# Weight halves made two blocks at a time: one ScalarE and one VectorE operation over two neighbouring blocks in the expert-mixture stage

## The chip, the cores and the metric

The kernel runs on one core of a Trainium2 chip. The metric is the device time in microseconds of one execution; the times shown are medians over runs of the same program. The profile is of one execution and is read in microseconds from the start of its span.

## What is computed

The whole kernel is two model blocks on 256 tokens of width 1024. The change is in the last stage, a mixture of 8 experts in which each token is sent to its best two:

```python
def moe_swiglu(h, router, wg, wu, wd):
    t = h.reshape(B_ * S_, D_)
    logits = (t @ router).astype(jnp.float32)
    top_v, top_i = lax.top_k(logits, TOP_K)
    gates = jax.nn.softmax(top_v, axis=-1)
    gate_full = jnp.sum(jax.nn.one_hot(top_i, N_EXPERTS, dtype=jnp.float32) * gates[..., None], axis=1)
    out = jnp.zeros_like(t)
    for e in range(N_EXPERTS):
        out = out + gate_full[:, e:e + 1].astype(t.dtype) * swiglu(t, wg[e], wu[e], wd[e])
    return out.reshape(B_, S_, D_)
```

`swiglu(h, wg, wu, wd)` is `(silu(h @ wg) * (h @ wu)) @ wd`, with 1024 x 3584 gate and up weights and 3584 x 1024 down weights for each expert, all float32.

## The kernel before

`stage_moe` works in passes. A pass gathers the rows of up to 128 tokens of one expert and streams that expert's weights from memory. There are `NE` = 8 passes and, for an expert with more than 128 tokens, an extra one; nine run with these inputs. A pass has 7 groups of 512 hidden columns; each group has 4 gate, 4 up and 4 down blocks, so `PASS` = 84 blocks of 128 x 1024 floats (512 KB). `ORDER` sets their order: gate 0, up 0, then for each further group g: gate g, up g, down g-1, and at last down 6. Blocks 80 to 83 are down 6.

A float32 product is made of three matmuls in the faster format `F32R`: each operand is split into a high half and the rest. For the weights this is done on the chip. `SP` loads a block into `raw`, a ring of `RING` = 21 slots. ScalarE's `high` (line 3610) copies it to `hi`, rounded, and VectorE's `low` (line 3783) writes `raw - hi` to `lo`. Both halves have `HALVES` = 6 buffers. TensorE (lines 3543 for gate and up, 3561 for down) reads them in 6 matmuls of 512 columns a block and adds one to `used`. `hi_ready`, `lo_ready` and `used` count blocks: `high` of block n waits for its load and for `used` of block n-6, `low` waits for `hi_ready`, TensorE and the reload of the ring slot wait for `lo_ready`.

Each engine runs its own program, in the order in which it is written. Between the halves stand the steps that tie groups together. ScalarE: `silu` writes `sg` (line 3625, with a load of its function table in the first group of a pass), `turned` writes `ah` (3629), `outputs` writes `y` (3636), `gathered` writes `hEh` (3620). VectorE: `product` writes `prod` (3788), `turned` writes `al` (3792), `places` (3815 to 3819, once a pass, after the up blocks of group 1, with two operations of 3737 behind it), `gathered` writes `hEl` (3778). TensorE: `turn` transposes `prod` (3550) and `down` waits for `al`; `who` (3531) stands between gate 0 and up 0; a pass's first matmul waits for `hEl`. The first `PRE` = 2 blocks of a pass are prepared at the end of the pass before: on ScalarE and VectorE block 0 of the next pass stands ahead of the last group's `turned`, block 1 behind it.

Of the kernel before, what the change touches and what calls it, by code (L numbers as in the profile page):

```python
# [7 lines left out]
ACT = mybir.ActivationFunctionType  # L8
ALU = mybir.AluOpType
# [9 lines left out]
T = 256  # L19
# [2092 lines left out]
HALVES = (slice(0, HD), slice(HD, P))  # L2112
# [1254 lines left out]
def stage_moe(nc, k, choice, w, hT, xn, x_tok, rows, out):  # L3367
# [10 lines left out]
    KINDS, UNITS = 3, 4  # L3378
    GATE, UP, DOWN = range(KINDS)
# [5 lines left out]
    PASS = GROUPS * KINDS * UNITS  # L3385
    RING, HALVES, PRE = 21, 6, 2
    ORDER = [(GATE, 0), (UP, 0)]
    for g in range(1, GROUPS):
        ORDER += [(GATE, g), (UP, g), (DOWN, g - 1)]
    ORDER.append((DOWN, GROUPS - 1))  # L3390
    AT_UNIT = {what: n * UNITS for n, what in enumerate(ORDER)}
    with Stage(nc, "moe") as st:
        sb, ps, sem = st.sb, st.ps, st.sem
        raw = sb("raw", [P, RING, D])
        hi, lo = sb("hi", [P, HALVES, D], F32R), sb("lo", [P, HALVES, D], F32R)
# [9 lines left out]
        hrow, gidx, gidx_ready, h_loaded = sb("hrow", [P, D]), sb("gidx", [P, 1], U32), sem("gidx_ready"), sem("h_loaded")  # L3405
# [4 lines left out]
        chosen, first, second = sb("chosen", [P, TT, NE]), sb("first", [P, TT, NE]), sb("second", [P, TT, NE])  # L3410
# [33 lines left out]
        with nc.Block() as block:  # L3444
# [157 lines left out]
            @block.scalar  # L3602
            def _(act):
                act.nop().then_inc(silu_ready, 1)
                act.activation(xh[:], xn[:], ACT.Copy).then_inc(xh_ready, 1)

                def high(p, n):
                    act.wait_ge(raw_loaded[n % RING], p * (PASS // RING * 16) + (n // RING * 16 + 16))
                    act.wait_ge(used, p * PASS + n + 1)
                    act.activation(hi[:, n % HALVES], raw[:, n % RING], ACT.Copy).then_inc(hi_ready, 1)  # L3610

                for n in range(PRE):
                    act.wait_ge(raw_loaded[n], 16)
                    act.activation(hi[:, n], raw[:, n], ACT.Copy).then_inc(hi_ready, 1)
                act.wait_ge(d_ready, 1)
                act.activation(e[:], df[:], ACT.Exp).then_inc(e_ready, 1)

                def gathered(p):
                    act.wait_ge(gather_psum, 2 * p + 2)
                    act.activation(hEh[:].rearrange("p k t -> p (k t)"), pX[:].rearrange("p b n -> p (b n)"), ACT.Copy).then_inc(hEh_ready, 1)  # L3620

                def silu(p, g):
                    act.wait_ge(used, AHEAD_USED + p * PASS + (AT_UNIT[GATE, g] + UNITS))
                    act.wait_ge(prod_ready, p * GROUPS + g + 1)
                    act.activation(sg[:], pB[:, GATE], ACT.Silu).then_inc(silu_ready, 1)

                def turned(p, g):
                    act.wait_ge(t_psum, p * GROUPS + g + 1)
                    act.activation(ah[:], pT[:], ACT.Copy).then_inc(ah_ready, 1)  # L3629

                def outputs(p):

                    act.wait_ge(used, AHEAD_USED + p * PASS)
                    act.wait_ge(y_free, p + 1)
                    act.wait_ge(idx_ready, p + 1)
                    act.activation(y[:].rearrange("p (h n) -> p h n", h=2), pY[:], ACT.Identity, scale=tokg[:, 1:2]).then_inc(y_ready, 1)

                def one(p):
                    for n in range(PRE, PASS):
                        high(p, n)  # L3640
                        if n == UNITS:
                            outputs(p)
                        kind, g = ORDER[(n - UNITS - 1) // UNITS]
                        if n >= 2 * UNITS and (n - UNITS - 1) % UNITS == UNITS - 1 and kind == GATE:
                            silu(p, g)
                            if g:
                                turned(p, g - 1)
                    high(p + 1, 0)
                    turned(p, GROUPS - 1)
                    for n in range(1, PRE):  # L3650
                        high(p + 1, n)
                    gathered(p + 1)

                act.wait_ge(gather_psum, 1)
                act.activation(hEh[:, 0:KD // 2].rearrange("p k t -> p (k t)"), pX[:, 0], ACT.Copy).then_inc(half_ready, 1)
                act.wait_ge(gather_psum, 2)
                act.activation(hEh[:, KD // 2:KD].rearrange("p k t -> p (k t)"), pX[:, 1], ACT.Copy).then_inc(hEh_ready, 1)

                def last(p):
# [37 lines left out]
            def _(dve):  # L3697
# [50 lines left out]
                for n in range(PRE):  # L3748
                    dve.wait_ge(hi_ready, n + 1)
                    dve.tensor_tensor(lo[:, n], raw[:, n], hi[:, n], ALU.subtract).then_inc(lo_ready, 1)  # L3750

                c.tick(dve.tensor_scalar(over[:], slot[:, :, 0:NE], float(P), None, ALU.subtract))
                c.link(dve.tensor_copy(wides[:], wide[:]))
# [24 lines left out]
                    dve.tensor_tensor(hEl[:].rearrange("p k t -> p (k t)"), pX[:].rearrange("p b n -> p (b n)"),  # L3778
                                      hEh[:].rearrange("p k t -> p (k t)"), ALU.subtract).then_inc(h_ready, 1)

                def low(p, n):
                    dve.wait_ge(hi_ready, p * PASS + n + 1)
                    dve.tensor_tensor(lo[:, n % HALVES], raw[:, n % RING], hi[:, n % HALVES], ALU.subtract).then_inc(lo_ready, 1)  # L3783

                def product(p, g):
                    dve.wait_ge(silu_ready, p * GROUPS + g + 2)
                    dve.wait_ge(used, AHEAD_USED + p * PASS + (AT_UNIT[UP, g] + UNITS))
                    dve.tensor_tensor(prod[:], pB[:, UP], sg[:], ALU.mult).then_inc(prod_ready, 1)

# [21 lines left out]
                def places(p):  # L3811

                    dve.wait_ge(m_psum, p + 1)
                    dve.wait_ge(y_free, p + 2)
                    dve.tensor_copy(tokg[:], pM[:, 0:3]).then_inc(ch2, 1)
                    dve.wait_ge(ch2, 2 * p + 1)
                    dve.scalar_tensor_tensor(out=idxf[:], in0=tokg[:, 2:3], scalar=unfilled[:, 1:2], in1=tokg[:, 0:1], op0=ALU.mult, op1=ALU.add).then_inc(ch2, 1)
                    dve.wait_ge(ch2, 2 * p + 2)
                    dve.tensor_tensor(idx[:], idxf[:], unfilled[:, 0:1], ALU.add).then_inc(idx_ready, 1)

                def one(p):
                    for n in range(PRE, PASS):
                        low(p, n)
                        kind, g = ORDER[(n - UNITS) // UNITS]
                        if n >= UNITS and kind == UP and (n - UNITS) % UNITS == UNITS - 1:
                            product(p, g)
                            if g == 1:
                                places(p)
                                gather_matrix(p + 1)
                            if g == 3:  # L3830
                                dve.wait_ge(a_psum, p + 1)
                                dve.tensor_scalar(gidx[:], pM[:, 4:5], float(T - 1), None, ALU.min).then_inc(gidx_ready, 1)
                        kind, g = ORDER[(n - UNITS - 1) // UNITS]
                        if n > UNITS and g and kind == GATE and (n - UNITS - 1) % UNITS == UNITS - 1:
                            turned(p, g - 1)
                    low(p + 1, 0)
                    turned(p, GROUPS - 1)

                    def others():
                        for n in range(1, PRE):  # L3840
                            low(p + 1, n)
                    gathered(p + 1, others)

                choices()
# [435 lines left out]
```

## Time and profile before

| | |
|---|---|
| median of 3 runs | 3125.44 us |
| lowest and highest of them | 3112.82 and 3127.72 us |
| span of the profiled execution | 3118.3 us |
| busy in the span: TensorE, weight loads, VectorE, ScalarE | 95%, 79%, 75%, 56% |
| mean granted TensorE clock | 0.974 |

The profile gives the profiled execution's span alone, from its first to its last instruction; it has no separate device time, so the span is what stands for it, and it is 7.1 us below the median of the runs. The halves are split from 2008.9 us on, and the last matmuls that read them start at 3107.8 us: the expert mixture is the last third of the span. TensorE's busy time is made of matmuls that overlap (a matmul of 512 columns lasts 0.39 us, the next one starts some 0.23 us after it), so a stall is best seen in what an engine waited for.

### The profile page before, as it was taken

To read this page: it belongs to the slowest core of one execution; us is meant where nothing else is said; L and a number is where in the kernel's file an instruction comes from. 1 tells how busy PE (TensorE), PEld (TensorE's weight loads), DVE (VectorE), ACT (ScalarE), POOL (GpSimd) and SP (SyncE) were. 2 spreads that over 40 slices of the span, in tenths; PEclk is the share of its full clock that TensorE was granted. 3 is DMA by queue.
4 is the path that set the end of the run, shared out by engine and by line. 5 is a ranking of instruction groups with operands and counts; after the bars stand their busy time and mean duration, and the time that the engine had idled before them with its cause. 6 is when DMAs were issued, how large, how long until landed. Compare 5 with 4: busy or idle time off the path is not lost. (4 is left out here: it accounts for less than half of the span.)

```text
span 3118.3 us, 52434 instructions
## 1 busy us (share of the span) xinstructions
PE 2962.4 (95%) x18296; PEld 2464.1 (79%) x18297; DVE 2341.3 (75%) x3606; ACT 1735.2 (56%) x2188; POOL 61.8 (2%) x69
## 2 busy tenths in 40 slices
PE   7999898999999999988899988899999999999999
PEld 3796547889888999977779877688888888888887
DVE  5675754889788666666655567699999998998998
ACT  4354303336533444446344363388888888888886
POOL 0000000000000000000000000000000000000000
PEclk9999899999999999999899998899999999999999
DMA  8570323444777666642145231499999999999995
GB/s 307 212 253 20 130 120 97 147 158 183 271 250 227 220 205 212 205 152 85 56 173 194 87 128 57 161 412 412 382 372 374 375 374 373 376 381 364 389 372 212
DMA packets 228409, 738.75 MB, mean 237 GB/s; under 512 B 23783, under 2 KB 60056, under 8 KB 225432
## 3 DMA queue, kind: packets, MB, share of 16 engines
q1 hardware_dynamic: 222648, 704.49, 61.7%
q0 software_dynamic: 5312, 31.98, 3.3%
q8 instruction: 85, 1.39, 0.2%
q14 instruction: 76, 0.62, 0.1%
q10 hardware_dynamic: 288, 0.26, 0.0%
HBM read 707.28 MB, written 29.36 MB: 236 GB/s over the span
## 5 line engine op out<-in xcount | busy, mean ns | idle before, releaser
L3783 DVE TENSOR_TENSOR moe_lo<-moe_raw,moe_hi 128x1024 fp32r<-128x1024 f32 x756 | 887.5, 1222 | 66.7 <-ACT moe_hi L3610 47.6
L3610 ACT ACTIVATE moe_hi<-moe_raw 128x1024 fp32r<-128x1024 f32 x756 | 791.0, 1061 | 155.4 <-PE moe_pB L3543 89.3
L3543 PE MATMUL moe_pB<-moe_hi,moe_hEh 128*128 128x512 f32 x1008 | 399.2, 396 | 0.3 <-DVE moe_hEl L3848 0.3
L3543 PE MATMUL moe_pB<-moe_hi,moe_hEl 128*128 128x512 f32 x1008 | 393.1, 390 | 0.0
L3543 PE MATMUL moe_pB<-moe_lo,moe_hEh 128*128 128x512 f32 x1008 | 392.7, 390 | 0.0
L3543 PEld LDWEIGHTS moe_pB<-moe_hi,moe_hEl 128*128 128x128 f32 x1008 | 189.3, 188 | 41.0
L3543 PEld LDWEIGHTS moe_pB<-moe_hi,moe_hEh 128*128 128x128 f32 x1008 | 189.3, 188 | 39.3 <-issue 1.7
L3543 PEld LDWEIGHTS moe_pB<-moe_lo,moe_hEh 128*128 128x128 f32 x1008 | 189.5, 188 | 37.6
L3561 PE MATMUL moe_pB<-moe_hi,moe_ah 128*128 128x512 f32 x504 | 197.1, 391 | 5.6 <-DVE moe_al L3792 5.6
L1971 PE MATMUL exp_pO<-exp_vh,exp_ah 128*128 128x512 f32 x512 | 200.1, 391 | 1.8 <-DVE exp_al L2056 1.8
L1971 PE MATMUL exp_pO<-exp_vl,exp_ah 128*128 128x512 f32 x512 | 200.0, 391 | 0.0
L1971 PE MATMUL exp_pO<-exp_vh,exp_al 128*128 128x512 f32 x512 | 199.2, 389 | 0.0
L3561 PE MATMUL moe_pB<-moe_hi,moe_al 128*128 128x512 f32 x504 | 196.3, 389 | 0.0
L3561 PE MATMUL moe_pB<-moe_lo,moe_ah 128*128 128x512 f32 x504 | 196.1, 389 | 0.0
L1996 ACT ACTIVATE exp_vh<-value_ring 128x1024 fp32r<-128x1024 f32 x128 | 134.7, 1055 | 103.5 <-PE exp_pO L1971 81.6
L2045 DVE TENSOR_TENSOR exp_vl<-value_ring,exp_vh 128x1024 fp32r<-128x1024 f32 x128 | 156.4, 1222 | 30.5 <-ACT exp_vh L1996 28.6
L2005 ACT ACTIVATE exp_ge<-exp_pS 128x256 f32<-128x256 f32 x64 | 24.5, 383 | 217.7 <-PE exp_pS L1959 217.7
L1959 PE MATMUL exp_pS<-fh,exp_ul 128*128 128x256 f32 x512 | 144.9, 283 | 0.0
L1959 PE MATMUL exp_pS<-fl,exp_uh 128*128 128x256 f32 x512 | 144.9, 283 | 0.0
L1959 PE MATMUL exp_pS<-fh,exp_uh 128*128 128x256 f32 x512 | 144.5, 282 | 0.0
L1621 PE MATMUL route_pS<-fh,route_uh 128*128 128x256 f32 x416 | 122.7, 295 | 8.4 <-DVE route_ul L1730 8.1
L2052 DVE TENSOR_TENSOR exp_at<-exp_ge,exp_gs 128x256 f32<-128x256 f32 x64 | 27.3, 426 | 128.5 <-ACT exp_ge L2005 114.6
(814 smaller groups left out, 6641.3 us busy)
## 6 DMA issues: line engine op xcount, KB each, us to landing
moe_raw<-in_moe_w SPq DMA_DIRECT2D x758, 512.0 KB, 6.5
value_ring<-in_peer_v SPq DMA_DIRECT2D x128, 512.0 KB, 4.4
key_ring<-in_peer_u SPq DMA_DIRECT2D x64, 512.0 KB, 3.6
exp_us<-in_peer_u SPq DMA_DIRECT2D x64, 512.0 KB, 5.1
inp_w<-in_w_mod SPq DMA_DIRECT2D x48, 512.0 KB, 7.6
inp_w<-in_w_tiles SPq DMA_DIRECT2D x40, 512.0 KB, 6.2
gates<-route_big POOLq DMA_DIRECT2D x8, 2048.0 KB, 7.3
exp_gs<-gates SPq DMA_DIRECT2D x32, 512.0 KB, 5.7
```

The lines of the kernel that those rows point to most:

```text
L1621: m = pe.matmul(pS[:, n % 2, 0:T], w, x[:, kd], start=kd == 0 and q == 0, stop=kd == KD - 1 and q == 2)
L1959: m = pe.matmul(pS[:, j % 2, 0:T], w, x[:, kd], start=kd == 0 and q == 0, stop=kd == KD - 1 and q == 2)
L1971: m = pe.matmul(pO[:, a, h], w[:, j % RING, ts], x, start=False, stop=False, skip_group_check=True)
L1996: act.activation(vh[:, j % RING], vs[:, j % RING], ACT.Copy).then_inc(vh_ready, 1)
L2005: act.activation(ge[:, j % 2], pS[:, j % 2, 0:T], ACT.Gelu).then_inc(ge_ready, 1)
L2045: dve.tensor_tensor(vl[:, j % RING], vs[:, j % RING], vh[:, j % RING], ALU.subtract).then_inc(vl_ready, 1)
L2052: dve.tensor_tensor(at[:].rearrange("p (c t) -> p c t", c=runs), scored.rearrange("p (c t) -> p c t", c=runs), gs[:, j // 4, :, j % 4], AL ...
L3543: i = pe.matmul(pB[:, kind], l[:, kd], m[:, n % HALVES, ns], start=kd == 0 and x == 0, stop=kd == KD - 1 and x == 2)
L3561: i = pe.matmul(pY[:, h], l[:, u], m[:, n % HALVES, hs], start=g == 0 and u == 0 and x == 0, stop=g == GROUPS - 1 and u == UNITS - 1 and x ...
L3610: act.activation(hi[:, n % HALVES], raw[:, n % RING], ACT.Copy).then_inc(hi_ready, 1)
L3783: dve.tensor_tensor(lo[:, n % HALVES], raw[:, n % RING], hi[:, n % HALVES], ALU.subtract).then_inc(lo_ready, 1)
```

## The change

`SPANS` cuts a pass into pairs of neighbouring blocks. Two blocks make a pair where both slots of `raw` and both buffers of `hi` and `lo` lie side by side, that is where neither ring wraps between them. A pass gets 40 pairs and 4 singles (blocks 20, 23, 62 and 65). One `high` and one `low` work on the whole span: `high` waits for both loads and for `used` of the span's last block less six, and the semaphores go up by two at its end. What stood behind a block now stands behind its span. At the end of a pass both first blocks of the next one are a pair behind `turned`. TensorE's program and that of `SP` are as they were.

```diff
+    SPANS, n = [], 0
+    while n < PASS:
+        both = n % RING < RING - 1 and n % HALVES < HALVES - 1
+        SPANS.append((n, 2 if both else 1))
+        n += SPANS[-1][1]
...
-                def high(p, n):
-                    act.wait_ge(raw_loaded[n % RING], p * (PASS // RING * 16) + (n // RING * 16 + 16))
-                    act.wait_ge(used, p * PASS + n + 1)
-                    act.activation(hi[:, n % HALVES], raw[:, n % RING], ACT.Copy).then_inc(hi_ready, 1)
+                def high(p, span):
+                    n, count = span
+                    for b in range(n, n + count):
+                        act.wait_ge(raw_loaded[b % RING], p * (PASS // RING * 16) + (b // RING * 16 + 16))
+                    act.wait_ge(used, p * PASS + n + count)
+                    act.activation(hi[:, n % HALVES:n % HALVES + count], raw[:, n % RING:n % RING + count], ACT.Copy).then_inc(hi_ready, count)
...
-                    for n in range(PRE, PASS):
-                        high(p, n)
-                        if n == UNITS:
-                            outputs(p)
...
-                    high(p + 1, 0)
+                    for first, count in SPANS[1:]:
+                        high(p, (first, count))
+                        for n in range(first, first + count):
+                            if n == UNITS:
+                                outputs(p)
...
                     turned(p, GROUPS - 1)
-                    for n in range(1, PRE):
-                        high(p + 1, n)
+                    high(p + 1, SPANS[0])
                     gathered(p + 1)
...
-                def low(p, n):
-                    dve.wait_ge(hi_ready, p * PASS + n + 1)
-                    dve.tensor_tensor(lo[:, n % HALVES], raw[:, n % RING], hi[:, n % HALVES], ALU.subtract).then_inc(lo_ready, 1)
+                def low(p, span):
+                    n, count = span
+                    dve.wait_ge(hi_ready, p * PASS + n + count)
+                    dve.tensor_tensor(lo[:, n % HALVES:n % HALVES + count], raw[:, n % RING:n % RING + count],
+                                      hi[:, n % HALVES:n % HALVES + count], ALU.subtract).then_inc(lo_ready, count)
...
-                    low(p + 1, 0)
                     turned(p, GROUPS - 1)
 
                     def others():
-                        for n in range(1, PRE):
-                            low(p + 1, n)
+                        low(p + 1, SPANS[0])
                     gathered(p + 1, others)
```

VectorE's program at the end of a pass, before: blocks 82 and 83 of the pass, block 0 of the next, the last `al`, block 1 of the next, `hEl`.

```order
L3783 TENSOR_TENSOR moe_lo<-moe_raw,moe_hi 128x1024
L3782 REGISTER_ALU
L3783 TENSOR_TENSOR moe_lo<-moe_raw,moe_hi 128x1024
L3782 ISA
L3783 TENSOR_TENSOR moe_lo<-moe_raw,moe_hi 128x1024
L3792 TENSOR_TENSOR moe_al<-moe_pT,moe_ah 128x512
L3774 ISA
L3782 REGISTER_ALU
L3783 TENSOR_TENSOR moe_lo<-moe_raw,moe_hi 128x1024
L3778 TENSOR_TENSOR moe_hEl<-moe_pX,moe_hEh 128x1024
```

The same place of the change: the pair 82 and 83, the last `al`, the pair 0 and 1 of the next pass, `hEl`.

```order
L3791 TENSOR_TENSOR moe_lo<-moe_raw,moe_hi 128x2048
L3801 TENSOR_TENSOR moe_al<-moe_pT,moe_ah 128x512
L3781 ISA
L3790 ISA
L3791 TENSOR_TENSOR moe_lo<-moe_raw,moe_hi 128x2048
L3785 TENSOR_TENSOR moe_hEl<-moe_pX,moe_hEh 128x1024
```

Of the three single `lo` ahead of the last `al`, the two of this pass have become one operation, and block 0 of the next pass has moved behind `al`.

VectorE's program of the change after the up blocks of group 1, behind the pair 18 and 19, `product` and the three operations of `places`: the two operations for `Pg`, single block 20, the pair 21 and 22, single block 23.

```order
L3745 TENSOR_SCALAR moe_Pg<-choice_io,moe_slot 128x128
L3745 REGISTER_ALU
L3745 TENSOR_SCALAR moe_Pg<-choice_io,moe_slot 128x128
L3790 REGISTER_ALU
L3791 TENSOR_TENSOR moe_lo<-moe_raw,moe_hi 128x1024
L3790 REGISTER_ALU
L3791 TENSOR_TENSOR moe_lo<-moe_raw,moe_hi 128x2048
L3790 REGISTER_ALU
L3791 TENSOR_TENSOR moe_lo<-moe_raw,moe_hi 128x1024
```

Before, the same steps stood between single blocks 19 and 20; now they stand between a pair and a single, with the next pair right behind.

## Rows read from the trace of the kernel before

**Rows 1.** The page's span and its busy time by engine, with share and instructions.

```profile
span 3118.3 us, 52434 instructions
...
PE 2962.4 (95%) x18296; PEld 2464.1 (79%) x18297; DVE 2341.3 (75%) x3606; ACT 1735.2 (56%) x2188; POOL 61.8 (2%) x69
```

**Rows 2.** 100 us in the MoE stage: each engine's busy time, clock, DMA.

```profile
2500.00:2600.00 100.00, 99.57 (x452) 82.49 (x453) 90.65 (x89) 83.11 (x86) 4.59 (x4) 1.00 0.98 369
```

**Rows 3.** Who waited for whom from 2100 to 3090 us: total us, times, longest.

```profile
ACT moe_hi L3610 <- PE moe_pB L3543: 82.9, 297, 0.3
...
DVE moe_lo L3783 <- ACT moe_hi L3610: 43.9, 89, 1.5
...
PE moe_pB L3561 <- DVE moe_al L3792: 5.0, 8, 0.6
```

**Rows 4.** Tile `moe_hi`, whole run: duration in ns (min/median/max), first and last start.

```profile
L3610 ACT ACTIVATE moe_hi<-moe_raw x756: 1043/1062/1069, 2024.0 to 3101.5; 128x1024 fp32r<-128x1024 f32 x189
L3783 DVE TENSOR_TENSOR moe_lo<-moe_raw,moe_hi x756: 1215/1222/1232, 2025.1 to 3102.5; 128x1024 fp32r<-128x1024 f32 x189
```

**Rows 5.** The page's group of `down`'s first matmuls: busy, mean ns, idle before and its releaser.

```profile
L3561 PE MATMUL moe_pB<-moe_hi,moe_ah 128*128 128x512 f32 x504 | 197.1, 391 | 5.6 <-DVE moe_al L3792 5.6
```

**Rows 6.** Tile `dense_uh` of the dense stage: the same two operations at 2048 columns.

```profile
L3963 ACT ACTIVATE dense_uh<-dense_us x21: 1903/1915/1917, 1594.3 to 1764.4; 128x2048 fp32r<-128x2048 f32 x21
L3993 DVE TENSOR_TENSOR dense_ul<-dense_us,dense_uh x21: 2291/2292/2293, 1596.2 to 1766.3; 128x2048 fp32r<-128x2048 f32 x21
```

**Rows 7.** The end of a pass: start us, duration us, engine, line, operation, idle before.

```profile
2492.89 0.39 PE L3561 MATMUL moe_pB<-moe_hi,moe_ah 128*128 128x512 f32 x1
...
2493.09 1.06 ACT L3610 ACTIVATE moe_hi<-moe_raw 128x1024 fp32r<-128x1024 f32 x1 [0.30 <-PE moe_pB L3543]
...
2498.34 0.60 PE L3550 MATMUL moe_pT<-ident,moe_prod 128*128 128x128 f32 x4
...
2498.97 0.60 ACT L3629 ACTIVATE moe_ah<-moe_pT 128x512 fp32r<-128x512 f32 x1 [0.73 <-PE moe_pT L3550]
...
2499.60 0.69 DVE L3792 TENSOR_TENSOR moe_al<-moe_pT,moe_ah 128x512 fp32r<-128x512 f32 x1
...
2500.43 0.49 PE L3561 MATMUL moe_pB<-moe_hi,moe_ah 128*128 128x512 f32 x1 [0.62 <-DVE moe_al L3792]
```

**Rows 8.** The turn of the same pass into the next one, the same columns.

```profile
2500.41 1.02 ACT L3620 ACTIVATE moe_hEh<-moe_pX 128x1024 fp32r<-128x1024 f32 x1
...
2501.45 1.28 ACT L3610 ACT_TABLE_LOAD   x1
...
2506.01 0.39 PE L3543 MATMUL moe_pB<-moe_hi,moe_hEh 128*128 128x512 f32 x1
...
2511.23 0.64 PEld L3531 LDWEIGHTS moe_pM<-moe_meta,moe_Pg 128*128 128x128 f32 x4
...
2511.81 0.49 PE L3543 MATMUL moe_pB<-moe_hi,moe_hEh 128*128 128x512 f32 x1
...
2513.01 0.60 ACT L3625 ACTIVATE moe_sg<-moe_pB 128x512 f32<-128x512 f32 x1
```

**Rows 9.** VectorE alone around `places` in the next pass, the same columns.

```profile
2528.97 0.69 DVE L3788 TENSOR_TENSOR moe_prod<-moe_pB,moe_sg 128x512 f32<-128x512 f32 x1 [0.29 <-PE moe_pB L3543]
...
2530.54 10.30 DVE L3783 TENSOR_TENSOR moe_lo<-moe_raw,moe_hi 128x1024 fp32r<-128x1024 f32 x9
```

**Rows 10.** The first blocks of the first pass, all engines, the same columns.

```profile
2024.03 2.96 ACT L3610 ACTIVATE moe_hi<-moe_raw 128x1024 fp32r<-128x1024 f32 x3 [0.95 <-PE moe_pB L3588]
...
2024.28 0.50 PE L3543 MATMUL moe_pB<-moe_hi,moe_hEh 128*128 128x512 f32 x1 [0.29 <-DVE moe_hEl L3848]
...
2025.12 3.50 DVE L3783 TENSOR_TENSOR moe_lo<-moe_raw,moe_hi 128x1024 fp32r<-128x1024 f32 x3 [1.08 <-ACT moe_hi L3610]
...
2027.13 0.39 PE L3543 MATMUL moe_pB<-moe_hi,moe_hEh 128*128 128x512 f32 x1
```

**Rows 11.** Tile `moe_raw`: from issue to landing of a block's load.

```profile
DMA to landing us min/median/max: 3.6/6.5/18.8
```

More of the change, by code:

```diff
@@ L3605, in _ @@
                 act.activation(xh[:], xn[:], ACT.Copy).then_inc(xh_ready, 1)
-                def high(p, n):
-                    act.wait_ge(raw_loaded[n % RING], p * (PASS // RING * 16) + (n // RING * 16 + 16))
-                    act.wait_ge(used, p * PASS + n + 1)
-                    act.activation(hi[:, n % HALVES], raw[:, n % RING], ACT.Copy).then_inc(hi_ready, 1)
+                def high(p, span):
[4 more added lines that the diff above has]
+                    act.activation(hi[:, n % HALVES:n % HALVES + count], raw[:, n % RING:n % RING + count], ACT.Copy).then_inc(hi_ready, count)
                 for n in range(PRE):
                     act.wait_ge(raw_loaded[n], 16)
-                    act.activation(hi[:, n], raw[:, n], ACT.Copy).then_inc(hi_ready, 1)
+                act.activation(hi[:, 0:PRE], raw[:, 0:PRE], ACT.Copy).then_inc(hi_ready, PRE)
                 act.wait_ge(d_ready, 1)
@@ L3638, in one @@
                 def one(p):
-                    for n in range(PRE, PASS):
-                        high(p, n)
-                        if n == UNITS:
-                            outputs(p)
[L3643 to L3647, printed above, removed]
-                    high(p + 1, 0)
+                    for first, count in SPANS[1:]:
[3 more added lines that the diff above has]
+                                outputs(p)
+                            kind, g = ORDER[(n - UNITS - 1) // UNITS]
+                            if n >= 2 * UNITS and (n - UNITS - 1) % UNITS == UNITS - 1 and kind == GATE:
+                                silu(p, g)
+                                if g:
+                                    turned(p, g - 1)
                     turned(p, GROUPS - 1)
-                    for n in range(1, PRE):
-                        high(p + 1, n)
+                    high(p + 1, SPANS[0])
                     gathered(p + 1)
@@ L3747, in _ @@
                 gather_matrix(0)
-                for n in range(PRE):
-                    dve.wait_ge(hi_ready, n + 1)
-                    dve.tensor_tensor(lo[:, n], raw[:, n], hi[:, n], ALU.subtract).then_inc(lo_ready, 1)
+                dve.wait_ge(hi_ready, PRE)
+                dve.tensor_tensor(lo[:, 0:PRE], raw[:, 0:PRE], hi[:, 0:PRE], ALU.subtract).then_inc(lo_ready, PRE)
                 c.tick(dve.tensor_scalar(over[:], slot[:, :, 0:NE], float(P), None, ALU.subtract))
@@ L3821, in one @@
                 def one(p):
[L3822 to L3835, printed above, removed]
-                    low(p + 1, 0)
+                    for first, count in SPANS[1:]:
+                        low(p, (first, count))
+                        for n in range(first, first + count):
+                            kind, g = ORDER[(n - UNITS) // UNITS]
+                            if n >= UNITS and kind == UP and (n - UNITS) % UNITS == UNITS - 1:
+                                product(p, g)
+                                if g == 1:
+                                    places(p)
+                                    gather_matrix(p + 1)
+                                if g == 3:
+                                    dve.wait_ge(a_psum, p + 1)
+                                    dve.tensor_scalar(gidx[:], pM[:, 4:5], float(T - 1), None, ALU.min).then_inc(gidx_ready, 1)
+                            kind, g = ORDER[(n - UNITS - 1) // UNITS]
+                            if n > UNITS and g and kind == GATE and (n - UNITS - 1) % UNITS == UNITS - 1:
+                                turned(p, g - 1)
                     turned(p, GROUPS - 1)
                     def others():
-                        for n in range(1, PRE):
-                            low(p + 1, n)
+                        low(p + 1, SPANS[0])
                     gathered(p + 1, others)
```

## Prediction

> **What bounds the kernel now.** I read the page first. The span is 3118.3 us and TensorE is busy for 95% of it [rows 1]. The MoE stage is the last third, so I read a stretch inside it: in 100 us TensorE is busy 99.57 us at a granted clock of 1.00 (its upper level, 2.4 GHz), VectorE 90.65 us and ScalarE 83.11 us [rows 2]. Busy shares can hide a wait, so the waits come next. Over 990 us ScalarE's `hi` waits for TensorE to give buffers back (297 times behind line 3543 alone, 82.9 us), while TensorE never waits for a `lo`. Its only listed wait for another engine is 0.6 us for `al`, once a pass [rows 3]; the page puts that wait at 5.6 us in all, over nine passes [rows 5]. TensorE sets the pace, and the halves arrive early. What ScalarE and VectorE save has no direct value; what counts is whether a pair is ready when TensorE comes to its first block.
>
> **The clock of the argument.** The last group's `turn` starts at 2498.34 and the four blocks ahead of it began at 2492.89 [rows 7], so a block takes 5.45/4 = 1.3625 us. ScalarE's `hi` starts 0.20 us after TensorE's next block does (2492.89 to 2493.09). `al` ends at 2500.29 and its first reader starts at 2500.43, so a result reaches TensorE in 0.14 us [rows 7]. The first `hi` of a pass runs 2024.03 to 2025.09 and its `lo` starts at 2025.12: 0.03 us [rows 10]. Single operations take 1.062 and 1.222 us [rows 4]. The operation on a pair is not in this stage before, but the dense stage has the same two instructions at 2048 columns: 1.915 and 2.292 us, with at most 2 ns above the median [rows 6]. I take those.
>
> **Part 1, fewer instructions.** A pass has 84 blocks: 40 pairs and 4 singles instead of 84 singles, on both engines. In isolation a pair saves VectorE 2 x 1.222 - 2.292 = 0.15 us, but nine back-to-back `lo` take 10.30 us [rows 9], a spacing of (10.30 - 1.22)/8 = 1.135, so two cost 2.27 us and a pair 2.292 - 0.085 = 2.21: 0.06 us saved, 360 x 0.06 = 22 us over the stage. None of it is on the path: cover is TensorE's 99.57%. Term: 0.
>
> The Trainium skill, Perfetto Trace Analysis, section Optimizing Scalar/DVE Operations, says larger operations help throughput if the engine is saturated, and that where ScalarE and VectorE are not saturated but hold others up, breaking instructions up can finish sooner. The rows above put this kernel on the second side; by that rule the change costs what the next parts find and earns nothing.
>
> **Part 2, the latency of a pair.** `hi` of blocks n and n+1 may start only when n-5 is used (six buffers); a single n needed n-6. The chain is 0.20 + 1.915 + 0.03 + 2.292 + 0.14 = 4.58 us. Between its start (block n-4 begins) and the need for block n lie four blocks, 5.45 us: 0.87 us to spare. Before it was 0.20 + 1.06 + 0.03 + 1.22 + 0.14 = 2.65 against five blocks, 6.81: 4.2 us to spare. So the steady pairs cost nothing, but the cover shrinks to 0.87 us, and I looked for the places where other work eats it.
>
> *End of a pass.* VectorE's `lo(82,83)` now stands ahead of the last `al`. Let `turn` start at t0 (2498.34). Block 77 ended at t0 - 2.73, so the pair's `hi` runs t0 - 2.53 to t0 - 0.61 and its `lo` t0 - 0.58 to t0 + 1.71. `al` can follow at t0 + 1.63 (0.085 overlap as above), ends at t0 + 2.32, and `down` of the last group starts at t0 + 2.46. Before it started at 2500.43, t0 + 2.09 [rows 7]. That is 0.37 us more a pass, 9 x 0.37 = 3.3 us. ScalarE's `ah` (ended t0 + 1.23) is not late.
>
> *The turn of a pass.* From `ah`'s end: `hi(0,1)` to t0 + 3.05, `hEh` (1.02 us [rows 8]) to t0 + 3.97, `lo(0,1)` t0 + 3.08 to 5.37, `hEl` to t0 + 6.5. TensorE starts the pass 5.58 us after `down` (2500.43 to 2506.01 [rows 7, 8]), so at t0 + 8.04: 1.4 us to spare. The table load (1.28 us [rows 8]) lets `hi(2,3)` start at t0 + 5.46 and its `lo` end at t0 + 9.69; block 2 is due at t0 + 10.8. Nothing. `silu(0)` needs a second load: counted from the pass's first block, `hi(8,9)` runs 5.65 to 7.57, the load to 8.85, `sg` to 9.45, `hi(10,11)` 9.35 to 11.27, `lo` to 13.6; block 10 is due at 10 x 1.3625 + 0.58 (the `who` matmuls, 2511.23 to 2511.81 [rows 8]) = 14.2. Nothing, 0.5 us to spare.
>
> *`al` of the other groups.* Count from the end of a group's gate blocks. `hi(n,n+1)` now runs ahead of `sg` from 0.20 to 2.12, `sg` and `ah` (0.60 each [rows 7, 8]) end by 3.3, `lo` runs 2.15 to 4.44, `al` (0.69 [rows 7]) 4.36 to 5.05, and its reader could start at 5.19. It is due after `turn` and four blocks, later than 5.45. Nothing, at least 0.26 us to spare.
>
> *After `places`.* Count from the start of block 14. `lo(18,19)` ends at 4.44, `product` starts at 4.36, and from `product` to the next `lo` is 1.57 us (2528.97 to 2530.54 [rows 9]), so single `lo(20)` starts at 5.93, `lo(21,22)` at 7.07 and ends at 9.36. With 0.14 that is 9.50; block 21 is due at 7 x 1.3625 = 9.54. This is a tie. Bounds: 0, or, if the chain is longer than I have it (ScalarE waits on three semaphores now, not two, and all of the present wait-to-start is 0.20, so at most about 0.2 more; below the rows there is no reason to go), some 0.16 us a pass, 1.4 us; the last `al` would then be 0.2 later too, 1.8 us. I take 0, which lies nearest to the rows.
>
> *First blocks of the first pass.* Here nothing is prepared beyond blocks 0 and 1. `hi(2,3)` starts at 2024.03 as before, ends 2025.95; `lo` ends 2028.27; TensorE can start block 2 at 2028.41. It started at 2027.13 [rows 10]. That is 1.3 us more, once.
>
> **Part 3, loads.** `SP` waits for the same counts of `lo_ready`, now in steps of two. A ring slot is freed at the latest when TensorE needs its block and refilled for a `hi` 17 blocks later, 23 us; landing takes 6.5 us, 18.8 at most [rows 11]. Term: 0.
>
> **Sum.** 3.3 + 1.3 = 4.6 us on the profiled span of 3118.3, so about 3122.9. That execution lies 7.1 us under the median of the three timed runs (3125.44), so the median becomes 3125.4 + 4.6 = 3130.0 us.
>
> **Rivals.**
> A. *Forecast*, 3128 to 3135: 0.72.
> B. *Nothing is lost.* The delayed `al` and the first blocks are caught up elsewhere: 3125. For it: 4.6 us is small. Against it: TensorE has no slack in which to catch up, 99.57 us of 100 [rows 2], and `hi` sits waiting for TensorE [rows 3], so it cannot come sooner. 0.10.
> C. *Faster: VectorE bounds after all.* Then 22 us (back to back) to 360 x 0.15 = 55 us come off: 3070 to 3103. For it: 90.65% busy. Against: no wait of TensorE for `lo` [rows 3]. 0.05.
> The Trainium skill, VectorE: DVE Perf Modes, section on the TRN2 errata, says a large tile pays the fixed SBUF latency once and small ones each time. That the 2048-column row is under two 1024-column rows agrees; by that rule alone it would be C.
> D. *Slower: the pair's chain is longer than four blocks.* It decides from 5.45 us on, 0.87 above my sum. Each 0.1 us beyond costs 40 x 9 x 0.1 = 36 us: 3161. For it: the chain is now two operations deep in one hand-over, and the margin falls by 3.3 us. Against: its pieces vary by hundredths [rows 4, 6]. 0.10.
> E. *Loads land late*, since slots come back in twos on queues kept near full [rows 2]. One block late a pass is 9 x 1.36 = 12 us: 3142. 0.03.
>
> **Numbers.** A change of 0.5%, 15.6 us, is about what a measurement of this kernel tells from none. A and B are within it (0.82), C is faster (0.05), D and E I count as slower (0.13). The runs shown spread over 14.9 us (3112.82 to 3127.72), so the range goes 14 us below the forecast; above it takes in E and the nearest part of D (a chain 0.05 us over, 18 us: 3148): 3116 to 3148.
>
> **What the profile after would show.** `lo` x360 at 2.29 us and x36 at 1.22; idle of VectorE before a pair near 0.43 us, of ScalarE near 0.8; TensorE's wait for `al` at line 3561 up from 5.6 to about 8.9 us; one new wait of 1.3 us for `lo` at block 2 of the first pass; none or hundredths before block 21 of each pass; busy TensorE still above 99 in each 100 us. Waits of TensorE for `lo` at every pair would mean D; a shorter stage with them absent would refute that TensorE sets the pace.

## The result and the profile after

| | before | changed |
|---|---|---|
| median, 4 runs each | 3124.39 us | 3137.55 us |
| lowest and highest | 3112.82 and 3127.72 us | 3134.54 and 3139.14 us |
| ratio | | 1.0047, 95% interval 1.0033 to 1.0062 |
| span of the profiled execution | 3118.3 us | 3137.3 us |

By the ratio the change costs 0.0047 x 3124.39 = 14.7 us, between 10.3 and 19.4. I had forecast 4.6 us. The median lies inside the stated range of 3116 to 3148 us, but above rival A's 3128 to 3135; the sign is the one that the sum had, and the size is three times it.

The page of the changed kernel, the lines that answer to [rows 1] and [rows 4]:

```profile
span 3137.3 us, 52020 instructions
...
PE 2973.7 (95%) x18296; PEld 2468.1 (79%) x18297; DVE 2307.8 (74%) x3245; ACT 1666.9 (53%) x1827; POOL 96.7 (3%) x69
...
L3791 DVE TENSOR_TENSOR moe_lo<-moe_raw,moe_hi 128x2048 fp32r<-128x2048 f32 (+1 forms) x396 | 863.8, 2193 | 144.4 <-ACT moe_hi L3619 143.3
L3619 ACT ACTIVATE moe_hi<-moe_raw 128x2048 fp32r<-128x2048 f32 (+1 forms) x396 | 724.6, 1838 | 245.6 <-PE moe_pB L3550 158.8
```

VectorE's and ScalarE's busy time fell, by 33.5 us and 68.3 us, and TensorE's did not: 2962.4 us before, 2973.7 us now, 95% of the span both times. In the 100 us from 2500 us on it is busy 98.58 us, where [rows 2] had 99.57. The mean of a `lo` is 2193 ns over pairs and singles.

The waits from 2100 to 3090 us, the lines that answer to [rows 3] (weight loads are listed apart as PEld, and wait together with the matmul behind them, so the two are not added):

```profile
PEld moe_pB L3568 <- DVE moe_lo L3791: 10.8, 8, 1.3
...
PE moe_pB L3568 <- DVE moe_al L3801: 8.9, 8, 1.1
PEld moe_pB L3550 <- DVE moe_lo L3791: 7.9, 16, 0.7
PE moe_pB L3550 <- DVE moe_lo L3791: 2.4, 8, 0.3
```

Before, the `al` line was 5.0 us, 0.6 at the most, and there was no line for `lo`. Now TensorE waits for `lo` too. To place the difference I took three starts from each trace: TensorE's first matmul of block 0 of the first pass, of `down` 6 in the first pass, and of `down` 6 in the last. They give the table's columns, all worked out from the timeline (the last one runs to the end of the span):

| us | stage | first pass to `down` 6 | one pass after that | from the last `down` 6 |
|---|---|---|---|---|
| before | 1094.0 | 114.95 | 120.40 | 15.85 |
| changed | 1110.5 | 120.02 | 121.63 | 17.50 |

The stage is 16.5 us longer. The other 2.5 us of the 19.0 between the spans had come about before its first matmul (2024.28 and 2026.81), in stages whose code is the same. Cutting one pass of both traces where TensorE changes its kind of work leaves three differences: the four gate blocks at its head 5.44 to 6.04 us, the gate blocks of group 2 (20 to 23) 5.44 to 5.60, and the stretch from the first transpose of the fetched rows to the last `down` 1.66 to 2.15. That is 0.60 + 0.16 + 0.49 = 1.25 us, against the 1.23 of the table (the last `down` itself is 0.02 shorter).

The end of a pass and the head of the next one in the changed kernel, the lines that answer to [rows 7, 8] (start us, duration us, engine, line, operation, idle before):

```profile
2506.67 1.92 ACT L3619 ACTIVATE moe_hi<-moe_raw 128x2048 fp32r<-128x2048 f32 x1 [0.80 <-PE moe_pB L3568]
...
2508.70 2.29 DVE L3791 TENSOR_TENSOR moe_lo<-moe_raw,moe_hi 128x2048 fp32r<-128x2048 f32 x1 [0.35 <-ACT moe_hi L3619]
...
2509.14 0.60 PE L3557 MATMUL moe_pT<-ident,moe_prod 128*128 128x128 f32 x4
...
2509.77 0.60 ACT L3638 ACTIVATE moe_ah<-moe_pT 128x512 fp32r<-128x512 f32 x1 [1.18 <-PE moe_pT L3557]
2510.27 1.90 ACT L3619 ACTIVATE moe_hi<-moe_raw 128x2048 fp32r<-128x2048 f32 x1
2510.91 0.68 DVE L3801 TENSOR_TENSOR moe_al<-moe_pT,moe_ah 128x512 fp32r<-128x512 f32 x1
...
2511.73 0.49 PE L3568 MATMUL moe_pB<-moe_hi,moe_ah 128*128 128x512 f32 x1 [1.12 <-DVE moe_al L3801]
...
2512.07 1.02 ACT L3629 ACTIVATE moe_hEh<-moe_pX 128x1024 fp32r<-128x1024 f32 x1
2512.27 2.29 DVE L3791 TENSOR_TENSOR moe_lo<-moe_raw,moe_hi 128x2048 fp32r<-128x2048 f32 x1 [0.68 <-ACT moe_hi L3619]
...
2514.48 1.22 DVE L3785 TENSOR_TENSOR moe_hEl<-moe_pX,moe_hEh 128x1024 fp32r<-128x1024 f32 x1
...
2514.82 1.28 ACT L3619 ACT_TABLE_LOAD   x1 [1.73 <-PE moe_pB L3568]
...
2516.11 3.72 ACT L3619 ACTIVATE moe_hi<-moe_raw 128x2048 fp32r<-128x2048 f32 x2
...
2518.13 4.49 DVE L3791 TENSOR_TENSOR moe_lo<-moe_raw,moe_hi 128x2048 fp32r<-128x2048 f32 x2 [2.43 <-ACT moe_hi L3619]
...
2520.48 0.50 PE L3550 MATMUL moe_pB<-moe_hi,moe_hEh 128*128 128x512 f32 x1 [0.30 <-DVE moe_lo L3791]
```

`turn` starts at 2509.14. The `lo` of blocks 82 and 83 ends at 2508.70 + 2.29 = 2510.99, and `al` (2510.91) stands behind it although `ah` has been there since 2510.37. That is the delay that the prediction had. The line it did not have is the table load: `hEh` ended at 2513.09, and the load starts at 2514.82, released by TensorE. Before, it started at 2501.45, 0.02 us after `hEh` ended [rows 8]. The first pair waits for three semaphores, two loads and `used`. In the trace of before the table load does not wait for `used`, only the `hi` behind it does; in the changed kernel all eight loads at the head of a later pass come 1.7 us late, released by TensorE, and the `hi` follows at once. So 1.28 us that had run inside a wait now follow it, the `lo` of blocks 2 and 3 ends at about 2520.4, and TensorE starts block 2 at 2520.48, 0.69 us after the matmul ahead of it and not 0.23.

The first blocks of the first pass, which answer to [rows 10]:

```profile
2026.73 1.28 ACT L3619 ACT_TABLE_LOAD   x1 [2.89 <-PE moe_pB L3595]
...
2026.81 0.49 PE L3550 MATMUL moe_pB<-moe_hi,moe_hEh 128*128 128x512 f32 x1 [0.16 <-issue]
...
2028.02 3.71 ACT L3619 ACTIVATE moe_hi<-moe_raw 128x2048 fp32r<-128x2048 f32 x2
...
2030.05 6.89 DVE L3791 TENSOR_TENSOR moe_lo<-moe_raw,moe_hi 128x2048 fp32r<-128x2048 f32 x3 [3.48 <-ACT moe_hi L3619]
...
2032.39 0.50 PE L3550 MATMUL moe_pB<-moe_hi,moe_hEh 128*128 128x512 f32 x1 [2.57 <-DVE moe_lo L3791]
```

Here too the load is late: it ends 1.20 us after block 0 has started, where before `hi` could start 0.25 us ahead of block 0 (2024.03 and 2024.28 [rows 10]). Block 2 starts 5.58 us after block 0, where it took 2.85 before. Three stretches behind it, with TensorE's granted clock as the last but two of the columns:

```profile
2029.40:2033.20 3.80, 1.23 (x5) 0.67 (x4) 3.15 (x2) 3.80 (x4) 0.38 (x1) 1.00 1.02 419
2033.20:2036.80 3.60, 3.60 (x10) 2.81 (x9) 3.50 (x2) 1.34 (x1) 3.42 (x2) 0.53 1.03 420
2036.80:2040.00 3.20, 3.20 (x17) 2.70 (x17) 1.00 (x2) 2.87 (x2) 1.69 (x1) 1.00 1.03 420
```

Over 3.6 us the mean granted clock is 0.53 (nearly all of it at the lower level, 1.2 GHz), right after a wait of 2.57 us, and it is back at 1.00 (the upper level, 2.4 GHz) after it. Before, it was 1.00 from 2030 to 2040 us.

After `places`, which answers to [rows 9]:

```profile
2542.41 0.68 DVE L3797 TENSOR_TENSOR moe_prod<-moe_pB,moe_sg 128x512 f32<-128x512 f32 x1
...
2543.97 6.76 DVE L3791 TENSOR_TENSOR moe_lo<-moe_raw,moe_hi 128x1024 fp32r<-128x1024 f32 x4
...
2547.45 0.19 PEld L3550 LDWEIGHTS moe_pB<-moe_hi,moe_hEh 128*128 128x128 f32 x1 [0.27 <-DVE moe_lo L3791]
...
2547.45 0.50 PE L3550 MATMUL moe_pB<-moe_hi,moe_hEh 128*128 128x512 f32 x1
...
2547.79 0.40 PE L3550 MATMUL moe_pB<-moe_lo,moe_hEh 128*128 128x512 f32 x1
```

`product` starts at 2542.41 and the next `lo` at 2543.97, 1.56 us later, as in [rows 9]. The four operations listed as one row are single 20, the pair 21 and 22, and what follows. Block 21 starts at 2547.45 and its second matmul 0.34 us after, not 0.23: the tie has gone slightly the wrong way.

### The profile page after: what moved, and what is told of

Read it like the earlier page. It is cut to its first block and busy times, and to the rows that moved or that the text cites. A ratio compares the mean times of both kernels' runs of the same rounds, so it can differ in the third digit from the quotient of the medians.

```text
span 3137.3 us, 52020 instructions
## 1 busy us (share of the span) xinstructions
PE 2973.7 (95%) x18296; PEld 2468.1 (79%) x18297; DVE 2307.8 (74%) x3245; ACT 1666.9 (53%) x1827; POOL 96.7 (3%) x69
## 5 line engine op out<-in xcount | busy, mean ns | idle before, releaser
L3791 DVE TENSOR_TENSOR moe_lo<-moe_raw,moe_hi 128x2048 fp32r<-128x2048 f32 (+1 forms) x396 | 863.8, 2193 | 144.4 <-ACT moe_hi L3619 143.3
L3619 ACT ACTIVATE moe_hi<-moe_raw 128x2048 fp32r<-128x2048 f32 (+1 forms) x396 | 724.6, 1838 | 245.6 <-PE moe_pB L3550 158.8
```

What stands on the lines that cost most here:

```text
L3619: act.activation(hi[:, n % HALVES:n % HALVES + count], raw[:, n % RING:n % RING + count], ACT.Copy).then_inc(hi_ready, count)
L3791: dve.tensor_tensor(lo[:, n % HALVES:n % HALVES + count], raw[:, n % RING:n % RING + count], hi[:, n % HALVES:n % HALVES + count], ALU.sub ...
```

## The experiments

Theory T: TensorE sets the pace, and the change costs what it does at four places: the table load behind the first pair's waits (each pass, and once more in the first), the wait and low clock of the first pass, `al` behind the last pair, block 21. Rival R1: pairs are slower everywhere, or the difference is in other stages. Rival R2 (C of the prediction): VectorE bounds, and its saved time shows once the waits are gone. Each ratio is to the kernel before on the same chip. In experiments 1 to 7 it lies 0.0001 to 0.0012 above what the traces' stages give (their excess over 1094.0 us, divided by the time before), though each interval holds that value; all seven are above the upper end of what I expected. The time alone seldom decides between theory and rival here, so the readings rest on the traces.

**1. The table load ahead of the waits (`early_load`).** An operation on one column (`spare`), which waits for nothing, stands at the head of a pass.

```diff
                 def one(p):
+                    act.activation(spare[:], k.zero[:, 0:1], ACT.Copy)
                     for first, count in SPANS[1:]:
```

> The changed kernel with a one-column copy of constants at the head of each pass on ScalarE, with no wait, so that ScalarE's table load (1.28 us) can run ahead of the wait for block 81. Theory (the load stands behind that wait and delays the first pair of each pass): the 0.46 us wait at block 2 of passes 1 to 8 goes, with its pipeline restart 0.57 us each, 4.6 us; in the first pass the wait at block 2 shrinks from 2.6 to about 1.3 us and the stretch at the lower clock behind it goes too, some 3 us. In all 7 to 8 us less than the changed kernel, ratio to before about 1.002. The wait for al stays at 1.12 us. Rival (the load's place does not matter, pairs are slow everywhere or the difference lies in other stages): ratio stays at 1.004 to 1.005 and the waits at block 2 stay.

Measured: 1.0033 (1.0021 to 1.0045), above the 1.002 that I expected; the interval reaches the rival's 1.004, so the trace has to decide. Stage 1101.0 us, a pass 121.0. The gate blocks at a pass's head take 5.44 us again. TensorE's waits over the stage:

```profile
PE moe_pB L3569 <- DVE moe_al L3803: 10.0, 9, 1.1
...
PEld moe_pB L3551 <- DVE moe_lo L3793: 4.0, 10, 1.6
...
PE moe_pB L3551 <- DVE moe_lo L3793: 1.2, 1, 1.2
```

The wait at block 2 is left in the first pass alone, 1.2 us, and the clock after it stays up:

```profile
2026.50:2028.50 2.00, 0.78 (x4) 0.42 (x3) 2.00 (x2) 2.00 (x3) 0.04 (x1) 1.00 1.03 422
2028.50:2031.00 2.50, 2.50 (x14) 2.01 (x12) 2.39 (x2) 1.68 (x1) 2.31 (x2) 1.00 1.02 419
```

`al` is as late as in the changed kernel. Of the 9.5 us by which the stage is shorter than the changed one, 1.6 are in its end (below); 7.9 are the term.

**2. `al` ahead of the last pair (`al_first`).**

```diff
-                    for first, count in SPANS[1:]:
+                    for first, count in SPANS[1:-1]:
                         low(p, (first, count))
...
                     turned(p, GROUPS - 1)
+                    low(p, SPANS[-1])
```

> The changed kernel with VectorE's last al of a pass put ahead of its last pair (blocks 82 and 83), which TensorE needs two blocks later. Theory (al is late because it stands behind a pair): TensorE's wait for the last al falls from 1.12 to 0.62 us, as in the kernel before, 9 x 0.5 = 4.5 us; up to 0.15 us a pass may come back at the start of the next pass, as hEl is later by 1 us. Ratio to before about 1.003 to 1.004. Rival (ah or the transposes are late, not VectorE): the wait stays near 1.1 us.

Measured: 1.0046 (1.0030 to 1.0061), where I expected 1.003 to 1.004. By time alone this is not told from the changed kernel. The trace tells it (stage 1104.5 us):

```profile
PEld moe_pB L3550 <- DVE moe_lo L3791: 9.5, 18, 2.9
...
PE moe_pB L3568 <- DVE moe_al L3801: 5.6, 9, 0.6
...
PE moe_pB L3550 <- DVE moe_lo L3791: 2.4, 1, 2.4
```

The wait for `al` is at its old 5.6 us, so VectorE's order made it late; a pass takes 121.15 us, 0.48 less than 121.63. The waits for `lo` stay, with 2.4 us at block 2 of the first pass, where the granted clock again falls to 0.53 for 3.6 us.

**3. Blocks 2 and 3 as singles (`head_singles`).**

```diff
-        both = n % RING < RING - 1 and n % HALVES < HALVES - 1
+        both = n % RING < RING - 1 and n % HALVES < HALVES - 1 and n not in (2, 3)
```

> The changed kernel with blocks 2 and 3 of each pass as singles. Each then has two waits, as before, and the table load no longer carries the wait for TensorE. Theory: the waits at block 2 go in all passes (8 x 0.57 us) and in the first pass both the wait of 2.6 us and the lower clock after it go, 1.7 us: about 9 us less than the changed kernel, ratio to before about 1.0015 to 1.002; al still 1.12 us. Rival (general slowness of pairs, 36 of the 40 pairs of a pass being as they were): ratio 1.004 to 1.005.

Measured: 1.0024 (1.0014 to 1.0033), which keeps out the rival's 1.004. Stage 1101.3 us, 9.2 less than the changed one; 115.84 to `down` 6 in the first pass, 120.99 a pass.

```profile
PE moe_pB L3568 <- DVE moe_al L3801: 10.0, 9, 1.1
...
PEld moe_pB L3550 <- DVE moe_lo L3791: 2.8, 11, 0.3
```

One pair of forty taken apart gives back 9.2 of the stage's 16.5 us. That speaks against R1.

**4. Both (`head_and_al`).** The edits of 2 and 3.

> Both: blocks 2 and 3 as singles, and the last al ahead of the pair 82 and 83. Theory: 9 + 4 us less than the changed kernel, ratio to before 1.000 to 1.001, with only the 0.1 us at block 21 of each pass left; span of the stage within 3 us of before. Rival (TensorE limits nothing and VectorE's saved time should show once the waits are gone): 10 us or more below before, ratio under 0.997. Rival (general slowness): above 1.003.

Measured: 1.0017 (1.0007 to 1.0028). Stage 1096.8 us, 2.8 over before; a pass 120.71.

```profile
PE moe_pB L3568 <- DVE moe_al L3801: 5.6, 9, 0.6
...
PEld moe_pB L3550 <- DVE moe_lo L3791: 2.8, 11, 0.3
```

No gain over the kernel before appears, so R2 falls. The time is a little above the expected ratio; the trace accounts for 2.8 us, 0.0009, which its interval holds.

**5. Pairs on ScalarE alone (`hi_pairs`).** VectorE's loops run over single blocks, ScalarE's stay.

```diff
-                    for first, count in SPANS[1:]:
+                    for first, count in [(n, 1) for n in range(PRE, PASS)]:
                         low(p, (first, count))
...
-                        low(p + 1, SPANS[0])
+                        for n in range(PRE):
+                            low(p + 1, (n, 1))
```

> ScalarE works in pairs as in the change, VectorE in single blocks, with the last al still behind blocks 82 and 83. Theory (places): al still late, TensorE's wait for it 1.1 us a pass, since VectorE starts blocks 82 and 83 only when the pair's hi is there; no wait at block 2 of passes 1 to 8, since lo of block 2 no longer waits for that of block 3 (1.07 us earlier, and the wait was 0.46); a wait of 1.7 us at block 2 of the first pass. Stage 6 to 8 us over before, ratio 1.002 to 1.0025. Rival (the pair on VectorE is what costs): ratio 1.000 to 1.001.

Measured: 1.0029 (1.0018 to 1.0040). Stage 1101.5 us, 7.5 over before; a pass 120.87.

```profile
PE moe_pB L3568 <- DVE moe_al L3801: 10.0, 9, 1.1
...
PEld moe_pB L3550 <- DVE moe_lo L3791: 1.8, 1, 1.8
```

`al` is late by the pair of `hi` alone, and the one wait for `lo` is in the first pass, though the table load still waits for TensorE. The clock stayed at 1.00 after it (the matmul itself waited 1.35 us; the 1.8 are the weight load's).

**6. Pairs on VectorE alone (`lo_pairs`).** The same edit on ScalarE's `high`, with its order of before at the end of a pass.

> VectorE works in pairs as in the change, ScalarE in single blocks in the order of before, so that its first operation of a pass has two waits and the table load is free of them. Theory: hi of block 82 is made 1 us before that of block 83, so the pair's lo ends 0.8 us sooner and al waits for ah alone (0.6 us, as before); nothing at block 2 of passes 1 to 8 or at block 21; in the first pass a wait of 1.3 us at block 2. Stage 1 to 3 us over before, ratio 1.0003 to 1.001. Rival (the pair on VectorE is what costs): ratio 1.003 or more.

Measured: 1.0012 (0.9999 to 1.0024). A pass takes 120.37 us, that of before within 0.03, and 116.35 to the first `down` 6 against 114.95. The one line for `al`:

```profile
PE moe_pB L3568 <- DVE moe_al L3802: 5.6, 9, 0.6
```

So pairs on VectorE alone cost 1.4 us once, the 1.3 us that the prediction had for the first blocks. Pairs on ScalarE alone cost 0.47 us a pass, all at the last `al`. The other two places need both: the gate blocks at a pass's head take 5.44 us in either of the two kernels and those of group 2 5.44 and 5.45, against 6.04 and 5.60 with pairs on both. Of the 1.23 us a pass, 0.47 come with ScalarE's pairs and 0.76 only with pairs on both.

**7. The kernel before with a late table load (`before_late_load`).**

```diff
                 def one(p):
+                    act.wait_ge(used, p * PASS + PRE + 2)
                     for n in range(PRE, PASS):
                         high(p, n)
```

> The kernel before (single blocks) with one wait added at the head of each pass on ScalarE, for the same count of used blocks that the first pair of the change waits for, so that the table load stands behind it. Theory (a late load costs only because pairs had used up the slack; singles have 3 to 4 us): no wait at block 2 of passes 1 to 8; up to 0.6 us at the start of the first pass; ratio 1.000 to 1.0005. Rival (a late load costs by itself): 0.5 us or more a pass, 4.6 us in all.

Measured: 1.0010 (0.9998 to 1.0023), which by itself would also hold the rival's 4.6 us (0.0015). The trace decides: the load starts 2.2 us late, released by TensorE, and a pass takes 120.40 us, that of before. To the first `down` 6 it is 115.78, 0.83 more, where I had expected up to 0.6. The late load costs nothing a pass by itself. It needs the pairs, which had used up the slack.

**8. One buffer less, pairs (`five_pairs`).**

```diff
-        AHEAD_LO, AHEAD_USED = RING, HALVES
+        AHEAD_LO, AHEAD_USED = RING, HALVES - 1
```

> The changed kernel as if hi and lo had five buffers, not six: every wait of ScalarE for used blocks is one block stricter. A pair's chain from TensorE's release to the first use (4.6 to 4.75 us) then has three blocks of cover, 4.09 us, in place of four. Theory (steady pairs are safe only by the 0.7 to 0.87 us that six buffers leave): TensorE waits at every pair; two pairs take 1.36 + 4.7 us and not 5.45, 0.3 us a pair more, 40 x 9 x 0.3 = 110 us; ratio 1.03 to 1.04. Rival (the chain is much shorter than I have it from the rows, or TensorE is not what limits): no change against the changed kernel, ratio 1.004 to 1.005.

Measured: 1.0532 (1.0507 to 1.0556), 166 us; I had 110, and 1.03 to 1.04.

```profile
PEld moe_pB L3568 <- DVE moe_lo L3791: 92.6, 63, 2.7
PEld moe_pB L3550 <- DVE moe_lo L3791: 75.1, 136, 2.9
PE moe_pB L3568 <- DVE moe_al L3801: 64.7, 54, 2.5
PE moe_pB L3550 <- DVE moe_lo L3791: 30.5, 67, 2.5
```

Steady pairs are safe by their sixth buffer only, as worked out. What I had left out is the line for `al`: 54 waits, 1.2 us each, or 64.7 us in all, in the other groups too. There `al` stands behind a pair that is itself late. That the two sum to the whole is not shown.

**9. One buffer less, singles (`five_singles`).** The same edit in the kernel before.

> The kernel before, in single blocks, as if hi and lo had five buffers. Theory: a single's chain is 2.7 to 2.8 us against four blocks, 5.45 us, so nothing is late: ratio 0.999 to 1.001, where the same cut cost the pairs 5.3%. Rival (five buffers cost by themselves, whatever the size of an operation): ratio 1.03 or more.

Measured: 1.0033 (1.0021 to 1.0044), outside what I expected. The blocks themselves are not late: all groups of blocks in a pass are within 0.04 us of before, but for one last `down` of 7.21 us (below). The rest is at one place:

```profile
PE moe_pB L3561 <- DVE moe_al L3792: 16.0, 9, 1.8
```

On ScalarE `hi` of the next pass's block 0 stands ahead of the last `ah`, and with five buffers it waits for block 79, so `ah` and `al` come later: 2.82 us from the first fetched transpose to `down` 6 and not 1.66. It is again an operation queued ahead of the last `al`. Nine times 1.16 is 10.4 us, the 0.33% measured. Against 5.3% for pairs it is small, so five buffers as such do not explain experiment 8.

**10. Block 21 too (`head_al_21`).** Experiment 4 with `n not in (2, 3, 21, 22)`.

> The changed kernel with the last al ahead of the pair 82 and 83, and with blocks 2, 3, 21 and 22 of each pass as singles. Theory: the wait at block 21 (0.15 to 0.18 us a pass) goes; what was left of 0.3 us a pass falls to 0.2 or less (hEl and the first gate blocks, later by VectorE's order at the turn). Stage 1 to 2 us over before, apart from the last matmuls, which in some executions run 1.6 us slower. Ratio 1.000 to 1.001. Rival (pairs give a gain once their waits are gone): ratio under 0.998.

Measured: 1.0003 (0.9992 to 1.0014). A pass takes 120.56 us and group 2's gate blocks 5.44 again. The 0.16 us left are at the turn of the pass: 5.64 + 5.58 us for `down` 6 and gate 0, against 5.58 + 5.44, less some hundredths elsewhere. 38 of 40 pairs a pass are in place, and the time is that of before.

**11. The wait that TensorE did have (`early_turn`).** From the kernel before, in single blocks. `ah` and `al` get two buffers (`g % 2`; the room comes from `Pz`, which moves into `ah`), and the last `turn` goes into the `down` ahead of it:

```diff
                         i.then_inc(used, 1)
+                        if g == GROUPS - 2 and u == UNITS - 2:
+                            turn(p, GROUPS - 1)
...
                         down(p, g - 1)
-                    turn(p, GROUPS - 1)
                     fetched(p + 1, 0)
...
-                    high(p + 1, 0)
                     turned(p, GROUPS - 1)
+                    high(p + 1, 0)
...
-                    low(p + 1, 0)
                     turned(p, GROUPS - 1)
+                    low(p + 1, 0)
```

> The kernel before, in single blocks, with the last group's transposes ahead of the last of the four down blocks in front of them, ah and al in two buffers each, and the last ah and al ahead of the next pass's block 0 on ScalarE and VectorE. Theory (TensorE sets the pace, so only its own wait, 0.62 us for al once a pass, is there to be had): the wait for al goes, 9 x 0.6 = 5.6 us, ratio to before 0.998 to 0.9985. Rival (another wait takes its place, for example for the gathered rows or for lo of the first blocks): ratio 0.9995 to 1.0005.

Measured: 0.9977 (0.9966 to 0.9988), median 3114.39 us against 3121.53. Its page:

```profile
span 3107.3 us, 52434 instructions
...
PE 2957.9 (95%) x18296; PEld 2464.0 (79%) x18297; DVE 2339.0 (75%) x3606; ACT 1733.9 (56%) x2188; POOL 64.0 (2%) x69
```

The list of waits has no line for `al` any more. A pass takes 119.53 us, 0.87 less, and the stage 1086.2 us, 7.8 less. That is more than the listed wait of 0.62: from the first transpose of the fetched rows to `down` 6 it is now 0.79 us and not 1.66, because `down` starts before the last of these transposes has ended, where before it came 0.62 us after that end. This version beats both kernels, with VectorE as busy as before.

## Why the prediction was right, and where it fell short

**The number.** 3137.55 us is in the range because the range was 14 us wide on the low side for the spread of the runs and wide on the high side for D and E, neither of which happened. It is not in the interval that I gave 0.72 to, and lies in the gap between A (to 3135) and E (3142). The sum was 4.6 us where about 15 were lost. That the time lies in the range is owed to the range's width and not to the sum; the mechanism was right in part, as follows.

**What bounds: right.** TensorE sets the pace. VectorE gave up 33.5 us of busy time and nothing came off (experiments 4 and 10); taking TensorE's own wait of 0.62 us away shortened the pass by 0.87 (11).

**Part 1, no value in fewer instructions: right.** Experiments 3, 4 and 10 get time back by taking pairs apart (4 and 10 by the order of `al` as well), with more instructions. The rule of the Trainium skill that the prediction set against the change (Perfetto Trace Analysis, section Optimizing Scalar/DVE Operations), that where these engines are not saturated but hold others up smaller instructions may finish work sooner, agrees with that.

**Part 2, steady pairs: right.** In the passes no wait was seen at a pair that had nothing else queued ahead of it, and with one block less of cover (experiment 8) there were waits throughout. The size of that experiment was off, since it left `al` out.

**End of a pass: right place, size 0.49 and not 0.37 us.** The hand-over from the pair's `hi` to its `lo` took 0.11 us (2506.67 + 1.92 to 2508.70), where I had 0.03 from singles. The longer hand-over goes with VectorE's operation on 2048 columns: it is 0.10 in experiment 6 too, where `hi` works on single blocks, and 0.03 in experiment 5, where `lo` does. In the dense stage the operations of [rows 6] show both, 0.03 at 11 places and 0.10 at 10, so the cause stays open. The `hi` began 2.47 us ahead of `turn`, where I had 2.53. Nine times 0.49 is 4.4 us, and the wait for `al` came to 10.0 us in all, where I had said about 8.9. Experiment 2 confirms the mechanism.

**Turn of a pass: wrong.** The step reads "The table load (1.28 us [rows 8]) lets `hi(2,3)` start at t0 + 5.46". It took the load to follow `hEh` at once, as in the trace of before. With a third semaphore to wait for, the load took over the wait for `used` and ran 1.7 us later. My slack there was 10.8 - 9.69 - 0.14 = about 1.0 us, less than the 1.28 of the load. I had put 0 where 8 x 0.60 = 4.8 us were lost. I had noted the third wait (under *After `places`*), and priced only its own time. Experiments 1 and 3 show the cause, each in another way, and 7 shows that it needs the pairs.

**First blocks: mis-sized.** The failing step is "`hi(2,3)` starts at 2024.03 as before". 1.3 us was forecast, and the first pass took 5.07 us more, of which 0.49 and 0.14 are `al` and block 21: 4.4 us. The late load makes a wait of 1.3 into one of 2.6 us, and the lower clock behind it costs the rest. In experiment 1 both are gone: the wait is 1.23 us and block 2 starts 1.37 us later than before, which is the forecast term.

**After `places`: a tie called at 0.** It was 0.16 us a pass, 1.4 us, the upper bound that the prediction gave for it. Taking 0 at a tie of 9.50 against 9.54 was a choice that the rows did not settle.

**The sum.** 4.4 + 4.8 + 4.4 + 1.4 = 15.0 us, against 16.5 in the stage and 14.7 by the ratio. The last 1.6 us are from the last `down` 6 on: the final matmuls ran at a lower granted clock in this execution (a mean of 0.81 from 3125 to 3137 us, against 1.00 from 3108 to 3118 before). Profiles of kernels 3, 5, 6, 7 and 10 show the same 17.4 to 17.6 us there, those of before and of 1, 2, 4 and 11 15.8 to 15.9, with the same code (9 has 18.3). I leave it out of the change's cost; why it comes and goes stays open.

**Rivals.** None of them came out as written. B is out, as each late place has its row. C is out (4 and 10). D did not happen and is as near as said (8). E was not seen: no wait for a load is listed in the passes. Of the signs, "busy TensorE still above 99 in each 100 us" failed: it is 98.58.

## What to carry to other kernels

Here, fusing operations on engines that are not the bound bought nothing and spent cover. Count how long the fused chain is against the buffers' lead, and then look at each step that is queued behind the longer operation, for that step is late first. An operation that waits for one more semaphore can shift a wait onto the table load in front of it: in the compiled program, see on which instruction each wait stands. The gain was in the one wait that the bounding engine had, 0.6 us a pass in a list of small numbers, which gave back 0.87.

## What the runs showed of the hardware that was not expected

A wait of TensorE of 2.57 us (changed kernel) and one of 2.44 us (experiment 2) at the same place were followed by 3.6 us at a granted clock of 0.53, waits of 1.23 and 1.35 us there (experiments 1 and 5) by none. The length of a wait alone does not settle it. In experiment 8 TensorE waited 2.47 us for the last `al` in each of nine passes, and four of these waits were followed by such a stretch; in experiment 9 one of nine waits of 1.78 us was (a mean of 0.51 from 2637.0 to 2640.5 us), and that `down` took 7.21 us and not 5.57. So a wait of 1.78 us cost 1.6 us more through the clock once, and nothing the other eight times.

A table load of 1.28 us can come to stand behind a wait, and what it costs the `hi` behind it depends on that: nothing where it runs while the wait lasts, 1.28 us of delay where it follows it.
